# One exponential per tile in place of one per PSUM bank, in the softmax attention of a two-block kernel on Trainium2

## What is computed

```python
def gqa_block(q_blk, k, v):
    s = jnp.einsum('bkgqd,bksd->bkgqs', q_blk, k).astype(jnp.float32) * (HEAD_DIM ** -0.5)
    p = jax.nn.softmax(s, axis=-1)
    return jnp.einsum('bkgqs,bksd->bkgqd', p.astype(v.dtype), v)
```

## Time and profile before

| what | value |
|---|---|
| median of 3 runs | 2446.06 us (2445.66 to 2452.49) |
| profiled execution, first to last instruction (its span) | 2444.0 us |
| TensorE matmul busy in that span | 2216.2 us (91%) |
| VectorE, ScalarE, GpSimd busy | 1096.1, 802.1, 712.9 us |
| softmax attention, exponential of tile 1 to that of tile 63 | 377.27 to 600.96 us |

### The profile page before, as it was taken

How to read it: one execution, slowest core, us unless ns; L and a number is a source line. 1 busy time by engine, 2 the same in 40 slices (tenths; PEclk the granted TensorE clock), 3 DMA queues, 4 the chain that set the end, 5 groups by cost and what they waited for, 6 DMA issues and landing times.

```text
span 2444.0 us, 27898 instructions
## 1 busy us (share of the span) xinstructions
PE 2216.2 (91%) x10833; PEld 1829.6 (75%) x10833; DVE 1096.1 (45%) x1470; ACT 802.1 (33%) x1426; POOL 712.9 (29%) x548
## 2 busy tenths in 40 slices
PE   5989888999999966666999999997999999999996
PEld 4778668999777855556888888776888888878775
DVE  7245648898261088888222110336232323221433
ACT  5122217888141178885000000233122112111212
POOL 2312230000222322220233332223333333247762
PEclk8989999999999987777999999998999999999998
DMA  4122021010231100002111211233111111122332
GB/s 157 44 96 70 18 78 35 10 44 10 95 122 52 45 16 1 1 1 78 43 44 49 64 47 48 86 104 104 43 50 44 48 47 45 49 86 94 120 130 78
DMA packets 133594, 146.33 MB, mean 60 GB/s; under 512 B 5828, under 2 KB 105688, under 8 KB 133496
## 3 DMA queue, kind: packets, MB, share of 16 engines
q1 hardware_dynamic: 117655, 94.43, 12.7%
q10 hardware_dynamic: 15840, 50.54, 5.7%
HBM read 127.13 MB, written 17.83 MB: 59 GB/s over the span
## 4 chain that ended last, share of the span: by engine, by line
PE 55%; issue 24%; DVE 11%; ACT 4%; POOL 3%; DMA 2%; ACTq 1%; POOLq 0%; DVEq 0%
PE psum L469 18%; PE psum L470 18%; PE psum L471 18%; DVE softplus_part L1742 2%; POOL w_ring L403 2%; DVE softplus L1739 1%; DVE stick_w_t L1753 1%; DVE softplus L1744 1%; POOL w_ring L401 1%; PE psum L746 1%; DVE xn L1464 1%; ACT softplus_part L1226 0%; DMA w_staging<-in_w_out 0%; DVE h L1469 0%; ACT softplus_part L1222 0%
## 5 line engine op out<-in xcount | busy, mean ns | idle before, releaser
L400 POOL TENSOR_TENSOR w_ring<-w_staging,zero 128x8 fp32r<-128x8 f32 x174 | 42.1, 242 | 1523.3 <-PE psum L471 1504.8
L403 POOL TENSOR_TENSOR w_ring<-w_staging,w_ring 128x1024 fp32r<-128x1024 f32 (+1 forms) x174 | 435.5, 2503 | 14.5
L469 PE MATMUL psum<-ffn_in,w_ring 128*128 128x512 f32 x704 | 280.1, 398 | 11.1 <-DVE ffn_in L1469 11.1
L470 PE MATMUL psum<-ffn_in,w_ring 128*128 128x512 f32 x704 | 277.7, 395 | 0.0
L471 PE MATMUL psum<-ffn_in,w_ring 128*128 128x512 f32 x704 | 276.9, 393 | 0.0
L469 PE MATMUL psum<-h,w_ring 128*128 128x512 f32 x576 | 228.9, 397 | 4.8 <-DVE h L1469 3.4
L470 PE MATMUL psum<-h,w_ring 128*128 128x512 f32 x576 | 227.4, 395 | 0.0
L471 PE MATMUL psum<-h,w_ring 128*128 128x512 f32 x576 | 226.8, 394 | 0.0
L1875 DVE SCALAR_TENSOR_TENSOR up_buf<-psum,vectors,up_buf 128x1023 f32<-128x1023 f32 x44 | 56.4, 1283 | 309.4 <-ACT up_buf L1360 309.4
L401 POOL TENSOR_SCALAR w_ring<-w_staging 128x1016 fp32r<-128x1016 f32 (+1 forms) x174 | 185.1, 1064 | 0.0
L469 PEld LDWEIGHTS psum<-ffn_in,w_ring 128*128 128x128 f32 x704 | 132.6, 188 | 42.7 <-DVE ffn_in L1469 11.8
(11 more groups left out here) (266 smaller groups left out, 4920.8 us busy)
## 6 DMA issues: line engine op xcount, KB each, us to landing
w_staging<-in_w_in SPq DMA_DIRECT2D x58, 512.0 KB, 3.8
w_staging<-in_w_up SPq DMA_DIRECT2D x44, 512.0 KB, 3.8
w_staging<-in_w_down SPq DMA_DIRECT2D x44, 512.0 KB, 3.2
w_staging<-in_w_out SPq DMA_DIRECT2D x16, 512.0 KB, 3.8
x_again<-scratch_x ACTq DMA_DIRECT2D x16, 512.0 KB, 4.7
xin<-in_x ACTq DMA_DIRECT2D x8, 512.0 KB, 3.2
x_again<-in_x ACTq DMA_DIRECT2D x16, 256.0 KB, 2.7
scratch_x<-h ACTq DMA_DIRECT2D x8, 512.0 KB, 2.6
```

The source lines that it names most:

```text
L400: pool.tensor_tensor(WR[:, r, 0, w:width], WS[:, s, w:width], ZERO[:, :], ALU.add)
L403: pool.tensor_tensor(WR[:, r, 1, 0:width], WS[:, s, 0:width], plain(WR[:, r, 0, 0:width]), ALU.subtract).then_inc(S["w_split"], 1)
L469: pe.matmul(dst, sh, mh, start=first, stop=False)
L470: pe.matmul(dst, sh, ml, start=False, stop=False)
```

## The change

The three activations of a tile become one over a view of the three banks (`p b n`: partitions, three banks, 348 columns in each), with the output viewed likewise. It adds one to `sc_exp` where the three added three. So `scores(i)` waits once, ahead of its first matmul, for the whole exponential of tile i - 1; `turn_probs(i)` waits for the same event as before.

```diff
             for b in range(3):
-                if i:
-                    pe.wait_ge(S["sc_exp"], 3 * i - 2 + b)
+                if i and b == 0:
+                    pe.wait_ge(S["sc_exp"], i)
                 for x, k2 in enumerate((KHH, KLL)):
...
             def turn_probs(i):
-                pe.wait_ge(S["sc_exp"], 3 * i + 3)
+                pe.wait_ge(S["sc_exp"], i + 1)
...
                 act.wait_ge(S["sc_max"], i + 1)
-                for b in range(3):
-                    act.activation(PR[:, i % 2, KPART * b:KPART * (b + 1)], PB[:, b, 0:KPART], ACT.Exp,
-                                   bias=NB[:, i % 2:i % 2 + 1], scale=-1.0).then_inc(S["sc_exp"], 1)
+                act.activation(PR[:, i % 2, :].rearrange("p (b n) -> p b n", b=3), PB[:, 0:3, 0:KPART], ACT.Exp,
+                               bias=NB[:, i % 2:i % 2 + 1], scale=-1.0).then_inc(S["sc_exp"], 1)
```

## The result

The changed kernel takes 2467.38 us (median of 4 runs, 2465.56 to 2467.86); the kernel before took 2446.59 us (median of 4). The ratio is 1.008 with a 95% interval of 1.0066 to 1.0095, so it is slower by 20.8 us. The span of the profiled execution went from 2444.0 to 2466.0 us.

A forecast was written before the change was run, and what follows sets the result against it. TensorE was taken as the bound, giving way to a 3.81 us loop per tile; 12.5 + 0.55 - 0.30 = +12.8 us makes the span 2456.8, and the 2.06 us median offset gives 2458.9 us, range 2451 to 2470.

The forecast's parts named there:

- What bounds: Attention tiles: TensorE sets the pace at 3.608 us a tile; ScalarE, 85% busy, would gain only idle time.
- The exponential: ScalarE's merged activation over 1044 elements takes 1.14 us instead of 1.44, saving about 0.30 us a tile.
- Rival B: One activation over three banks saves nothing: 1.44 us, loop 4.11 us, 2477 us in all; chance 0.06.
- rival A: Not slower: exponential plus release under 1.13 us, loop 3.70 us, 2452 us, within 0.3%; chance 0.18.
- The release: Banks return to TensorE 0.07 us after the whole exponential, so next scores start 1.21 us after its start.
- The loop: Scores, hand-over, two copies, exponential and release sum to 3.81 us a tile instead of 3.608: +12.5 us.
- 0.96 us of scores: First term of the round: TensorE's six score matmuls run without a gap in 0.96 us.
- the signs that I had named: Included two tiles in 7.6 us, all six score matmuls without a gap, and scores waiting some 18 us in all.
- The pauses ahead of the scores: TensorE stands still 0.10 us before a long tile's scores and 0.46 before a short one's.
- The ends: Attention's edges: tile 1's scores start 0.55 us later, tile 63's transposes get the exponential 0.30 us earlier.
- rival C: TensorE's pauses lower the clock: three 20 us stretches give 2486 us, the whole attention stage 2660; chance 0.04.
- Behind the attention: Whatever follows the attention begins later by the same amount, and nothing there changes length.

The follow-up runs named there:

- short exponential: Changed kernel with its one activation computing only 116 of the 348 columns of each third, the rest preset to ones: 2442.61 us, ratio 0.9982.
- late wait: Kernel before, three activations per tile kept, but TensorE waits once, for the third, ahead of the first score matmul: 2487.78 us, ratio 1.0164.
- short copy: Changed kernel with ScalarE's second large copy of transposed probabilities cut to 128 of its 512 columns: 2456.78 us, ratio 1.0039.
- Two banks, then one: Kernel before with two activations per tile, over the first two banks and over the third, waits matched: 2450.05 us, ratio 1.0011.
- One bank, then two: Kernel before with two activations per tile, over the first bank and over the other two, waits matched: 2459.02 us, ratio 1.0046.
- the two with the swap: Changed kernel and kernel before, each with the exponential moved ahead of the previous tile's second large copy: 2494.68 us (1.019) and 2511.79 us (1.0265).
- changed, even product: Changed kernel with the product's 27 matmuls cut 14 and 13 instead of 15 and 12: 2467.27 us, ratio 1.0083.

## Why the prediction was right, and where it was short

- **What bounds.** Right: ScalarE's saved 0.30 us a tile bought nothing, and the bound went from TensorE to a loop. The short exponential and the late wait show both halves of it.
- **The exponential.** 1.14 us forecast from an element's price, 1.136 measured. Rival B is gone, and rival A with it.
- **The release.** 1.21 us from the exponential's start to the next scores forecast, 1.19 measured, in every tile; of it 0.05 is the release, not 0.07.
- **The loop.** Forecast 3.81 us (the terms add up to 3.805), measured 3.914, and so +19.0 us in the stretch, not +12.5. The order of the steps was right (copies last, minimum behind them: the short copy shows it). The term that was mis-sized is the first one, "0.96 us of scores": the dense value was taken for scores that begin behind a wait. In the changed kernel they take 1.05 to 1.06. That is 0.095 x 62 = 5.9 us of the 6.5 missing. The rows had shown it: in the earlier trace rows a matmul waits at 526.51 and the transposes follow at 526.93, 0.42 us later for two matmuls that take 0.32 dense. I booked it as waiting for the exponential; by the starts only 0.02 of the 0.17 us in these scores is waiting and 0.15 is that price. The rest: in 12 of the tiles the exponential starts 1.11 or 1.12 us after the first copy and not 0.97, 1.7 us in all; the kernel before has such tiles too, and I didn't find their cause. (Each of them starts behind the end of the second copy, the others 0.12 us ahead of it.) The shorter release takes 1.2 us back. Of the signs that I had named, two missed with that term: two tiles take 7.83 us and not 7.6, and the score matmuls do not lie without a gap. The pauses ahead of the scores came as forecast, 0.29 us a tile on average or 18 us in all by the starts; the table of waits books them as 10.2 us of matmuls and 20.9 of weight loads, so it isn't the place to read them.
- **The ends.** From tile 0's exponential to tile 1's 5.43 us (371.52 to 376.95) instead of 5.01: +0.42, forecast +0.55.
- **The clock.** 1.00 in the attention with pauses of 0.41 us in nearly every short tile (from its transposes at 528.13 to the scores at 530.93 it is 2.80 us, where the earlier trace rows have 2.39) and 0.25 in the long tile behind 524.08 (3.00 against 2.75): rival C didn't come. With three activations and one wait the pauses are up to 0.73 us, and from 390 us on the clock is 1.00 too. The rule of the Trainium skill that spoke for it ("TensorE: Matmul & The Clock Gate", A second HAM failure mode: psum-queue depth-cycling) shows no effect here.
- **Behind the attention.** Forecast: everything shifts by the same. The span grew by 22.0 us, 3 more than the stretch. From the first to the last activation that splits the feed-forward's middle it is 248.3 us before (2166.3 to 2414.6) and 250.9 after (2185.1 to 2436.0). One experiment has 251.4 there and all others 248.3 to 248.5, with or without the merged exponential, so I take these 2.6 us for scatter of that stage, which no run tests. The medians differ by 20.8, 19.1 of it from the attention and its edges.

The forecast of 2458.9 was 8.5 us too low and 2467.38 lies in the range of 2451 to 2470; the sign and the mechanism were right, the size nearly 40% short.

## What to carry to other kernels

Before merging instructions to save their fixed cost, ask who waits for the first piece: with one buffer between two engines, the merged instruction releases everything at its end, and a loop of dependences can become the bound while all engines are partly idle. Write down when the consumer asks for each piece and when the merged instruction gives it back, and merge only pieces that still come back in time. An early first release alone isn't enough. Two banks, then one, cost 0.1% here: the pair is back 0.90 us after the start and asked for at 0.79 or 1.09. One bank, then two, cost 0.5%, since the second bank, asked for at 1.11, is back at 1.34 only. All three in one cost 0.8%. When a chain is summed up, take the consumer's first instruction behind a wait at its price behind a wait, not at the dense one.

## What the runs showed of the hardware

A matmul that has to wait on a semaphore can cost up to 0.10 us beyond the wait, and the cost shows in the matmul behind it. How much it is depends on how far ahead of the matmul its weight load began. TensorE's weight loads and matmuls (start, length), dense and at the second bank of the short tile in the kernel before:

```profile
522.34 0.19 PEld L647 LDWEIGHTS psum<-k_hi_hi,q_stack 128*128 128x128 f32 x1
522.45 0.19 PEld L647 LDWEIGHTS psum<-k_lo_lo,q_stack 128*128 128x128 f32 x1
...
526.07 0.19 PEld L647 LDWEIGHTS psum<-k_hi_hi,q_stack 128*128 128x128 f32 x1
526.12 0.37 PE L647 MATMUL psum<-k_hi_hi,q_stack 128*128 128x348 f32 x1
526.33 0.32 PE L647 MATMUL psum<-k_lo_lo,q_stack 128*128 128x348 f32 x1
```

and behind a full wait in the changed kernel:

```profile
530.93 0.19 PEld L647 LDWEIGHTS psum<-k_hi_hi,q_stack 128*128 128x128 f32 x1 [0.43 <-ACT probs L1126]
530.93 0.42 PE L647 MATMUL psum<-k_hi_hi,q_stack 128*128 128x348 f32 x1 [0.23 <-ACT probs L1126]
531.04 0.19 PEld L647 LDWEIGHTS psum<-k_lo_lo,q_stack 128*128 128x128 f32 x1
531.19 0.32 PE L647 MATMUL psum<-k_lo_lo,q_stack 128*128 128x348 f32 x1
```

In the dense case the load stands at 522.34, 0.11 us ahead of its matmul at 522.45, under the matmul of the product. Behind the full wait load and matmul both begin at 530.93, though TensorE had stood idle: the load was not brought forward over the wait. The case in between is at 526.12: the matmul starts on time, its load only 0.05 us ahead of it, and the next matmul follows after 0.21 us. The short second copy shows where such a load begins: its exponential ends at 525.37, the load starts at 525.42 with the release, and the matmul at 525.50, when its turn has come.

The traces of eight kernels here (all but the two with the swap, "three activations, one wait" and "changed, even product") show 1303 first matmuls of a bank between 400 and 600 us, and they follow one line:

| load starts ahead of its matmul by | next matmul starts after |
|---|---|
| 0.00 us | 0.26 to 0.27 us |
| 0.02 us | 0.24 to 0.25 us |
| 0.05 us | 0.21 to 0.22 us |
| 0.07 us | 0.19 to 0.20 us |
| 0.09 us | 0.17 to 0.18 us |
| 0.11 us and more | 0.15 to 0.17 us |

So the next matmul starts some 0.27 us after the load, or at its dense 0.16 us if that is later. That gives the whole of the 0.10 us and its smaller values too. It is read from the traces of kernels that were changed for other ends; no run moved the load alone.
